# The end of a decoder step: combination and last LayerNorm, dealt out to three engines

## The reference, cut to what matters

```
f = _hier_moe(tok, ...)                 # row = wt[0] * expert_row[0] + wt[1] * expert_row[1]
xp = _layer_norm(ALPHA * xp + mod_p[5] * fp, ln2_g[l], ln2_b[l])
xs = _layer_norm(ALPHA * xs + mod_s[5] * fs, ln2_g[l], ln2_b[l])
# _layer_norm(x, g, b) = (x - mean) * rsqrt(var + 1e-5) * g + b, over the 1024 features
```

## Time and profile before

| what | us |
|---|---|
| median of 3 runs | 1174.28 |
| lowest and highest | 1171.39, 1175.01 |
| the profiled execution | 1169.97 |
| its span, first to last instruction | 1168.0 |
| VectorE busy in the span | 344.6 (30%) |
| ScalarE busy | 187.1 (16%) |
| GpSimd busy | 107.9 (9%) |
| TensorE busy | 878.8 (75%) |

### The profile page before, as it was taken

The page is one execution under the profiler, slowest core; times in us unless marked ns, Lnnn a source line. Parts: engine busy times, 40 slices in busy tenths (PEclk is TensorE's granted clock), DMA queues, the critical chain, the costliest instruction groups (busy, mean ns, idle before and its releaser), DMA issues.

```text
span 1168.0 us, 11688 instructions
## 1 busy us (share of the span) xinstructions
PE 878.8 (75%) x4564; PEld 480.1 (41%) x4564; DVE 344.6 (30%) x525; ACT 187.1 (16%) x449; POOL 107.9 (9%) x114
## 2 busy tenths in 40 slices
PE   6699999996666878999250787777777877778740
PEld 5584763785552334477240432222222322222210
DVE  2066995961423222132750100000000000000008
ACT  2312232211122111000320211111111110111110
POOL 1110111200001110200010010000000000000020
PEclk9799999999677777999665799999999899999985
DMA  9987785785597877999999399999999999999931
GB/s 317 396 292 283 294 311 202 302 299 185 182 382 310 325 309 288 353 384 379 381 328 349 146 426 426 425 426 425 425 425 425 426 425 425 426 425 425 425 136 59
DMA packets 64740, 396.30 MB, mean 339 GB/s; under 512 B 6194, under 2 KB 8774, under 8 KB 41479
## 3 DMA queue, kind: packets, MB, share of 16 engines
q1 hardware_dynamic: 50544, 307.46, 66.1%
q0 software_dynamic: 12016, 85.90, 19.5%
q10 hardware_dynamic: 2144, 2.44, 0.6%
HBM read 387.89 MB, written 58.10 MB: 382 GB/s over the span
## 4 chain that ended last, share of the span: by engine, by line
PE 50%; DMA 34%; DVE 8%; issue 3%; ACT 3%; SPq 1%; ACTq 1%; POOL 0%; POOLq 0%; DVEq 0%
DMA ring<-in_w_exp_up_dram 26%; PE bank L393 11%; PE bank L722 11%; PE bank L403 5%; PE bank L558 4%; PE bank L637 2%; DMA listed_tokens<-v,didx 2%; DMA ring<-in_w_in_dram 2%; DMA ring<-in_w_ada_dram 2%; PE bank L438 2%; PE bank L416 2%; PE bank L624 1%; PE bank L340 1%; PE bank L500 1%; PE bank L598 1%
## 5 line engine op out<-in xcount | busy, mean ns | idle before, releaser
L722 PE MATMUL bank<-ring,hT 128*64 128x512 f32 x1024 | 241.7, 626 | 45.0 <-DMA ring<-in_w_exp_up_dram 42.5
L722 PEld LDWEIGHTS bank<-ring,hT 128*64 128x64 f32 x1024 | 89.0, 143 | 196.4 <-issue 196.4
L1465 DVE TENSOR_TENSOR hT<-hT,bank 128x256 f32<-128x256 f32 x32 | 19.2, 601 | 414.9 <-ACT hT L1024 414.9
L393 PE MATMUL bank<-hT,ring 128*128 128x264 f32 x576 | 134.0, 393 | 3.2 <-DMA ring<-in_w_in_dram 3.2
L740 PE MATMUL bank<-ring,hT 128*64 128x512 f32 x512 | 118.6, 604 | 19.4 <-DVE hT L1468 19.4
L393 PEld LDWEIGHTS bank<-hT,ring 128*128 128x128 f32 x576 | 109.9, 193 | 23.6 <-issue 5.1
L1096 DVE TENSOR_TENSOR ring<-ring,qbc 128x4096 f32<-128x4096 f32 x16 | 70.7, 4419 | 50.0 <-ACTq L767 40.7
L1602 POOL DMA_INDIRECT expert_rows<-work,ridx x32 | 31.1, 973 | 481.7 <-ACT work L759 377.1
L740 PEld LDWEIGHTS bank<-ring,hT 128*64 128x64 f32 x512 | 40.9, 138 | 76.6 <-issue 76.6
L759 ACT ACTIVATE work<-bank 128x512 f32<-128x512 f32 (+5 forms) x91 | 38.1, 427 | 209.8 <-PE bank L740 144.3
L1100 DVE TENSOR_REDUCE S<-ring 128x64 f32<-128x4096 f32 x16 | 70.6, 4414 | 0.2
(11 more groups left out here) (295 smaller groups left out, 807.5 us busy)
## 6 DMA issues: line engine op xcount, KB each, us to landing
ring<-in_w_exp_up_dram SPq DMA_DIRECT2D x32, 2048.0 KB, 22.0
ring<-in_w_exp_down_dram SPq DMA_DIRECT2D x32, 2048.0 KB, 21.8
ring<-in_w_exp_gate_dram SPq DMA_DIRECT2D x32, 2048.0 KB, 17.6
out_dram<-in_state_dil_kv_dram SPq DMA_DIRECT2D x8, 4064.0 KB
ring<-in_w_ada_dram SPq DMA_DIRECT2D x12, 2048.0 KB, 12.8
ring<-in_w_in_dram SPq DMA_DIRECT2D x11, 2048.0 KB, 13.9
out_dram<-in_state_dil_kv_dram SPq DMA_DIRECT2D x8, 992.0 KB
ring<-in_state_dil_kv_dram POOLq DMA_DIRECT2D x6, 1024.0 KB, 7.0
```

The lines of the kernel that those rows point to most:

```text
L393: i = mm(bk[:, 0:NT], w[:, k, j * P:(j + 1) * P], hT3[:, k, :], start=(k == 0), stop=(k == KC - 1))
L722: i = mm(side(2, half).rearrange("p (m n) -> p m n", m=2), xT[s][:, k, :], w[:, :, k, half * 256:(half + 1) * 256], start=(k == 0), stop=( ...
```

## The change

The end is dealt out by tile and by engine. ScalarE multiplies `ya` by the first weight, for the tiles 0, 2, 1 in this order, as soon as a tile's first gather has landed; each gather has its own semaphore now, and tile 2's gathers are issued ahead of tile 1's. VectorE combines tiles 0 and 1 only, with three instructions each. The residual is multiplied by ALPHA earlier, on VectorE, ahead of the copies of the turned token list. GpSimd does tile 2: four instructions for its combination, and three for its normalization. Statistics of all tiles stay on VectorE, but spread, root and reciprocal are taken tile by tile, and the tiles' normalizations stand between other tiles' steps. SyncE waits for each tile's own semaphore, still in the order 0, 1, 2.

The semaphores of gathers and finished tiles:

```diff
-        s_gat = [sem(f"s_gat{t}") for t in range(3)]
+        s_gat = [sem(f"s_gat{i}") for i in range(6)]
+        s_yd = [sem(f"s_yd{t}") for t in range(3)]
```

ScalarE, behind the expert loop:

```diff
-            root(4)
+            for n, t in enumerate((0, 2, 1)):
+                tn = TT[t][1]
+                act.wait_ge(s_gat[2 * t], 16)
+                ya = ring[0:tn, t, 0:DM]
+                A(ya, ya, ACT.Identity, scale=wts[0:tn, t, 0:1]).then_inc(s_wa, 1)
+            for n, t in enumerate((0, 1, 2)):
+                act.wait_ge(s_var, 4 + n)
+                A(sdev[:, t:t + 1], sdev[:, t:t + 1], ACT.Sqrt).then_inc(s_sd, 1)
```

VectorE, ahead of the copies of the turned token list:

```diff
+            for t, (t0, tn) in enumerate(TT):
+                V.tensor_scalar(x[0:tn, t, :], x[0:tn, t, :], ALPHA, None, ALU.mult).then_inc(s_xa, 1)
```

VectorE, behind the expert loop:

```diff
-            for t, (t0, tn) in enumerate(TT):
-                ya, yb = ring[0:tn, t, 0:DM], ring[0:tn, t, DM:2 * DM]
-                xt = x[0:tn, t, :]
-                dve.wait_ge(s_gat[t], 32)
-                link(V.tensor_scalar(ya, ya, wts[0:tn, t, 0:1], None, ALU.mult))
-                link(V.scalar_tensor_tensor(ya, yb, wts[0:tn, t, 1:2], ya, ALU.mult, ALU.add))
-                link(V.tensor_tensor(ya, ya, g2p[0:tn, :] if t < 2 else g2s, ALU.mult))
-                link(V.scalar_tensor_tensor(xt, xt, ALPHA, ya, ALU.mult, ALU.add))
-            normalize([(x[0:tn, t, :], x[0:tn, t, :], tn) for t, (t0, tn) in enumerate(TT)], s_y, affine=True)
+            dve.wait_ge(s_xa, 3)
+            def combine(t):
+                ya, yb = ring[:, t, 0:DM], ring[:, t, DM:2 * DM]
+                dve.wait_ge(s_wa, (1, 3)[t])
+                dve.wait_ge(s_gat[2 * t + 1], 16)
+                link(V.scalar_tensor_tensor(ya, yb, wts[:, t, 1:2], ya, ALU.mult, ALU.add))
+                link(V.tensor_tensor(ya, ya, g2p, ALU.mult))
+                link(V.tensor_tensor(x[:, t, :], x[:, t, :], ya, ALU.add))
+            def spreads(t):
+                tn = TT[t][1]
+                link(V.bn_stats(stat[0:tn, 4:10], x[0:tn, t, 0:512]))
+                link(V.bn_stats(stat[0:tn, 10:16], x[0:tn, t, 512:DM]))
+                link(V.bn_aggr(nst[0:tn, t, :], stat[0:tn, 4:16]))
+                V.tensor_scalar(sdev[:, t:t + 1], nst[:, t, 1:2], EPS, None, ALU.add).then_inc(s_var, 1)
+            def roots(t):
+                dve.wait_ge(s_sd, 4 + t)
+                i = V.reciprocal(sdev[:, t:t + 1], sdev[:, t:t + 1])
+                if t < 2:
+                    link(i)
+                else:
+                    i.then_inc(s_t2, 1)
+            def normed(t):
+                xt = x[:, t, :]
+                link(V.scalar_tensor_tensor(xt, xt, nst[:, t, 0:1], lng, ALU.subtract, ALU.mult))
+                V.scalar_tensor_tensor(xt, xt, sdev[:, t:t + 1], lnb, ALU.mult, ALU.add).then_inc(s_yd[t], 1)
+            combine(0)
+            spreads(0)
+            combine(1)
+            roots(0)
+            normed(0)
+            spreads(1)
+            dve.wait_ge(s_t2, 1)
+            spreads(2)
+            roots(1)
+            roots(2)
+            normed(1)
```

GpSimd, the gathers and what stands behind them:

```diff
-            for t, (t0, tn) in enumerate(TT):
+            for t in (0, 2, 1):
+                tn = TT[t][1]
                 for i_ in range(2):
...
-                    ).then_inc(s_gat[t], 16)
+                    ).then_inc(s_gat[2 * t + i_], 16)
+            ya, yb, xt = ring[0:NB, 2, 0:DM], ring[0:NB, 2, DM:2 * DM], x[0:NB, 2, :]
+            G = nc.gpsimd
+            plink = chain(pool, s_pchain)
+            pool.wait_ge(s_gat[5], 16)
+            plink(G.tensor_scalar(yb, yb, wts[0:NB, 2, 1:2], None, ALU.mult))
+            pool.wait_ge(s_wa, 2)
+            plink(G.tensor_tensor(ya, ya, yb, ALU.add))
+            plink(G.tensor_tensor(ya, ya, g2s, ALU.mult))
+            pool.wait_ge(s_xa, 3)
+            G.tensor_tensor(xt, xt, ya, ALU.add).then_inc(s_t2, 1)
+            pool.wait_ge(s_t2, 2)
+            plink(G.tensor_scalar(xt, xt, nst[0:NB, 2, 0:1], sdev[0:NB, 2:3], ALU.subtract, ALU.mult))
+            plink(G.tensor_tensor(xt, xt, lng[0:NB, :], ALU.mult))
+            G.tensor_tensor(xt, xt, lnb[0:NB, :], ALU.add).then_inc(s_yd[2], 1)
```

SyncE, the stores:

```diff
-                sp.wait_ge(s_y, t + 1)
+                sp.wait_ge(s_yd[t], 1)
```

More of the change, by code:

```diff
@@ L205, in trunk @@
         s_rtab, s_idx, s_scat, = (sem(n) for n in "s_rtab s_idx s_scat".split())
-        s_y, s_out, s_st, s_vout, = (sem(n) for n in "s_y s_out s_st s_vout".split())
-        s_dve, s_pool, = (sem(n) for n in "s_dve s_pool".split())
+        s_xa, s_wa, s_t2, s_out, s_st, s_vout, = (sem(n) for n in "s_xa s_wa s_t2 s_out s_st s_vout".split())
+        s_dve, s_pool, s_pchain, = (sem(n) for n in "s_dve s_pool s_pchain".split())
         s_vread = [sem("s_vread0"), sem("s_vread1")]
         v_full = [sem(f"v_full{i}") for i in range(4)]
-        s_gat = [sem(f"s_gat{t}") for t in range(3)]
+        s_gat = [sem(f"s_gat{i}") for i in range(6)]
+        s_yd = [sem(f"s_yd{t}") for t in range(3)]
         s_kout = [sem("s_kout0"), sem("s_kout1")]
```

## The result

The change made the kernel slower. The median after is 1181.68 us (five runs, 1180.16 to 1182.62), before 1174.67 (five runs, 1171.39 to 1175.01). The ratio is 1.0062, with a 95% interval of 1.0046 to 1.0079: 7.3 us more, between 5.4 and 9.3. The forecast was 1176.5, at most 1180. The profiled execution of after took 1181.93 us, with a span of 1180.0; before, 1169.97 and 1168.0.

What follows compares the result with a forecast made beforehand. VectorE alone was taken to bound the last stretch; its end comes 8.05 us earlier, but seven GpSimd instructions of 1.72 nearly all return, so the span grows 2.25 and the median becomes 1176.5, range 1168.5 to 1180.

Steps and rivals of the forecast that it cites:

- the likeliest case: Tail: VectorE and GpSimd exclude each other, GpSimd instructions about 1.7 us, 8-row store last; median 1174 to 1178, chance 0.45.
- What VectorE loses and gains: Tail: VectorE's new list, undisturbed, runs from 1138.66 to the last reciprocal at 1155.16 and ends at 1157.76.
- ScalarE's part and the residual: Tail products on ScalarE, 1.06 to 1.25 us, hidden under gathers; residual's early multiplication in VectorE's idle time costs nothing.
- that rival: Before the token list's copies: the residual's multiplication holds the list by up to 0.75 us, median 1177.3; chance 0.05.
- its sign: Sign named for a wrong forecast: the token list landing later than 640.4.
- Exclusion, both ways: Tail: two-input VectorE instructions and GpSimd's SBUF reads keep each other out, whoever is first; applied to all seven GpSimd instructions.
- The delay to the last reciprocal: Tail: GpSimd's combination delays VectorE by 1.72, 1.62 and 1.72, 5.06 us in all, last reciprocal at 1160.22.
- I take 1.72 for all seven: Tail: each of GpSimd's seven 8x1024 instructions costs 1.72 us, drawn from prices at 32 and 64 columns.
- The rival without exclusion: Tail: VectorE undisturbed, GpSimd ends at 1160.51, span 5.3 us less, median 1169.0; chance 0.25.
- The lower bound of 0.24: Tail: GpSimd's two one-input instructions with constants might take only 0.24 us, as at 8 columns, without growth.
- The rival with dearer instructions: Tail: the same turns with GpSimd instructions of 1.94 us, 3.7 later than today, median 1178.0; chance 0.25.
- With 2.19 for the store: End of the span: 2.19 us added behind GpSimd's last instruction at 1168.06, giving a span of 1170.25.

Runs made afterwards that it cites:

- e4: The changed kernel without GpSimd's first four instructions, so the 8-row tile is not combined: median 1175.91 us, ratio 1.0014 against the kernel before.
- e7: The kernel before with only the residual's multiplication moved early and a plain addition at the end: median 1171.82 us, ratio 0.9983.
- e3: The kernel before plus GpSimd instructions during the token-list wait, alone, then beside VectorE products and statistics; only single durations count: two-tile sum 2.33 us alone.
- e1: The kernel before plus one 8x8 GpSimd instruction that waits for VectorE's last pass: median 1180.44 us, ratio 1.0047.
- e2: The kernel before plus the same 8x8 GpSimd instruction, waiting only for the first tile's last pass: median 1174.45 us, ratio 0.9998.
- e5: The changed kernel with the 8-row tile's normalization back on VectorE, its combination still on GpSimd: median 1172.2 us, ratio 0.9995 against the kernel before.
- e6: The changed kernel with the 8-row tile's combination and normalization on VectorE, no GpSimd arithmetic: median 1171.72 us, ratio 0.9992 against the kernel before.
- e8: The changed kernel without GpSimd arithmetic, and ScalarE taking sums and sums of squares of tiles 0 and 1: median 1169.15 us, ratio 0.9961 against before.

## Why the prediction was wrong

The mechanism was right as far as the last reciprocal: VectorE and GpSimd keep each other out, and GpSimd works last. The step that failed is the one from there to the end of the span. GpSimd's three instructions were priced too low, and its closing was not in the sum at all; the end comes with that closing, and not with the 8-row store, as the likeliest case had it.

- **What VectorE loses and gains: right.** 16.50 us from its first instruction to the last reciprocal, undisturbed, were forecast; e4 shows 16.23.
- **ScalarE's part and the residual: right.** The product took 1.15 us, between 1.06 and 1.25, and VectorE never waited for it; the root's table load (1146.74 to 1148.02) was done before it was wanted at 1149.94. The residual's multiplication cost nothing that can be measured (e7), and that rival falls. By the letter its sign came, since the list lands at 641.05 in after (616.82 + 24.23) and not by 640.4. But GpSimd's first write already starts 0.92 us later there (610.11, before 609.19), ahead of the multiplication, and the wait itself is the shorter one.
- **Exclusion, both ways: right, but not for all seven.** That VectorE would wait too rested, as far as the trace went, on GpSimd's waits in the earlier trace rows alone; the instructions of 3.25 us and e3 show it. The rule of the Trainium skill ("SBUF — State Buffer", section "Who interferes with whom"), that the two exclude each other and that whoever is first keeps the other out, holds here for sums and products of two tiles (VectorE 3.245 instead of 1.224), and for none of the statistics (0.694). That it lasts for the whole instruction does not hold for GpSimd's instructions with one input: one that takes 2.83 us alone held VectorE by 0.80, and the measurement decides. The rival without exclusion falls; it would have had VectorE at the last reciprocal after 16.5 us, where 21.27 passed.
- **The delay to the last reciprocal: the sum right, its parts not.** 5.06 forecast, 5.04 measured (e4). But it was 1.72 + 1.62 + 1.72 in the forecast and 0.80 + 0.19 + 2.02 + 2.01 in the trace. GpSimd's first instruction, with one input, held VectorE by 0.80 only, though its record is 3.67 long. It also began beside VectorE's first instruction and not behind its second, and only one of GpSimd's instructions, not two, ran under the statistics. The last two held VectorE by 2.0 each. That these errors cancel is chance.
- **"I take 1.72 for all seven": wrong, and with the turns behind it +1.83.** A price at 1024 columns was drawn from 32 and 64 columns. Two tiles took 2.33, one tile and one constant 2.79, one tile and two operations 3.77 (e3). The last three in the tail took 9.67 us where 7.84 (1160.22 to 1168.06) were forecast. That is the difference of two errors. The price alone is worth +3.27 (8.43 instead of 3 x 1.72 = 5.16). Against it, the forecast had GpSimd wait out both of VectorE's passes, 2.68 us (1.32 + 1.28 + 0.08); it waited 0.97 for the first only, beside 0.27 of gaps, since the second ran under GpSimd's first instruction, delayed by 0.82. The lower bound of 0.24 for the instructions with constants was off the most: these are the dearest (2.83 and 3.77). The rival with dearer instructions named the direction, at 1.94, and even that was too low. The estimate from the Trainium skill ("GPSIMD Engine Reference", section 3.1), 2.25 for a sum of two tiles, is near the 2.33 measured here; the kinds with one input are not in that figure.
- **"With 2.19 for the store": wrong, +3.45.** This is the larger part. The 2.19 us were taken over from before, and GpSimd's closing was put at nothing without a reason. In before the end did follow the store, because GpSimd had closed 22.8 us earlier (1145.2 against 1168.0). The store was sized right in after too: SyncE was through at 1176.4, 2.0 us behind GpSimd's last instruction. Once GpSimd is last, the end comes with its closing, 5.64 us behind its last instruction. e1 shows the term by itself (6.0 instead of 2.2 with an instruction of 0.24 us), e2 that it vanishes under cover, e5 that it goes when GpSimd is not last. No rival of the prediction held it.

The sum with what was measured: forecast +2.25 for the span; +1.83 for GpSimd's last three, +3.45 for the closing, +0.56 for the gathers, and -0.29 for VectorE (21.27 instead of 21.56) make +7.80, beside 7.8 in the tails of the profiles and 7.0 between the medians. The gathers' 0.56 and the smaller of these differences are within what executions differ by. The parts come apart in the experiments as well: without GpSimd's four instructions of the combination the tail is 43.1 (e4, 5.6 less than after), without its last three 41.1 (e5, 7.6 less).

What stays open: what GpSimd does in its closing was not tried. Shown is that it ends 5.4 us behind the last arithmetic instruction in five runs (after, e1, e2, e4, e5), whether that instruction takes 0.24 us or 3.20. Behind a gather's issue it varies more: 5.4 to 7.2 us in before, e6, e7 and e8.

## What to carry to other kernels

Ask of an engine that is given the last piece of work not only what the piece costs there but also how long that engine takes to close; in the trace of before, GpSimd's closing was to be read (1139.50 to 1145.2), it was only covered. A price should be measured at its own size before a chain is built on it, in a stretch where the engine is idle anyway. And two-input work on VectorE was not relieved by GpSimd but interrupted by it: GpSimd's combination of the 8-row tile cost VectorE 5.04 us (e4), and on VectorE itself the three instructions take 3.8 (e6). ScalarE ran beside VectorE without turns; with its help and no arithmetic on GpSimd the tail was 5.5 us shorter than before (e8).

## What the runs showed of the hardware that was not expected

- GpSimd's closing DRAIN ends 5.4 us behind its last arithmetic instruction (after 5.41; e1, e2, e4 and e5 5.4), SyncE's takes 13 ns and ScalarE's 8, and VectorE's (1165.9 + 2.14 after) ends within 0.1 us of its last instruction.
- On GpSimd a product with a constant (2.79 us) is dearer than a product of two tiles (2.33), and a second operation in the instruction costs 0.85 to 0.94 more (e3).
- A GpSimd instruction with one input let a waiting two-input VectorE instruction in early: one that takes 2.83 us alone delayed it by 0.80 us (1144.74, 2.02 instead of 1.22), and one that takes 3.77 by 0.82 (1165.91, 2.10 instead of 1.28).
